# Turning the memory rows of a cross-attention on VectorE and through DRAM, with the norm's root applied behind the projections

## What is computed

```python
def memory_cross_attention(h, m, w_q, w_kv, q_g, k_g, w_o):
    q = rmsnorm(heads(h @ w_q, MEM_HEL2614 TENSOR_TENSOR XL<-SMP,XH 128x4x128 [waits mixed_hi] x2
L2600 TENSOR_TENSOR MGAINED<-MEM,PRE_GAIN 128x512 [waits pre_gain_loaded,mem_loaded]
L2600 TENSOR_TENSOR MGAINED<-MEM,PRE_GAIN 128x512
L2603 STREAM_TRANSPOSE MEM_TURNED_92<-MGAINED 128x4x4x32 [waits mem_gained] x2
L2516 TENSOR_TENSOR XS<-ACCP,XS 128x512 [waits gate_ready,block_done]
...
L2600 TENSOR_TENSOR MGAINED<-MEM,PRE_GAIN 128x512 [waits pre_gain_loaded,mem_loaded]
L2600 TENSOR_TENSOR MGAINED<-MEM,PRE_GAIN 128x512
L2603 STREAM_TRANSPOSE MEM_TURNED_93<-MGAINED 128x4x4x32 [waits mem_gained] x2
L2234 TENSOR_TENSOR LO<-RAW,HI 128x1024 [waits hi_ready,x_again]
...
L2270 SCALAR_TENSOR_TENSOR XS<-X,STAT,POST_GAIN 128x512 [waits xq_gain_loaded,root_ready,acc_taken3,acc_taken2]
L2270 SCALAR_TENSOR_TENSOR XS<-X,STAT,POST_GAIN 128x512
L2674 TENSOR_TENSOR MLO<-MEM_TURNED_92,MH 128x4x128 [waits mem_hi] x2S), q_g)
    k, v = jnp.split(m @ w_kv, 2, axis=-1)
    k = rmsnorm(heads(k, MEM_HEADS), k_g)
    v = heads(v, MEM_HEADS)
    s = jnp.einsum("bqhd,bkhd->bhqk", q, k).astype(jnp.float32) * MEM_DIM ** -0.5
    p = jax.nn.softmax(s, axis=-1).astype(v.dtype)
    o = jnp.einsum("bhqk,bkhd->bqhd", p, v).reshape(B, S, MEM_W)
    return o @ w_o
...
x = x + mixed @ w_out[l]
x = x + memory_cross_attention(rmsnorm(x, norm_xq[l]), rmsnorm(mem, norm_mem[l]), ...)
```

## Time and profile before

| | |
|---|---|
| median of 3 runs | 1126.58 us (1126.37 to 1127.04) |
| the profiled execution | 1127.05 us, of which its span is 1125.1 us |
| PE busy | 1114.9 us, 99% of the span |
| PEld busy | 946.8 us, 84% |
| DVE busy | 766.9 us, 68% |
| ACT busy | 597.0 us, 53% |
| POOL busy | 107.6 us, 10% |
| granted clock of PE, mean | 0.998 of full speed |
| share of PE in the chain that ended last | 93% |

### The profile page before, as it was taken

The page is one execution under the profiler, slowest core; times in us unless marked ns, Lnnn a source line. Parts: engine busy times, 40 slices in busy tenths (PEclk is TensorE's granted clock), DMA queues, the critical chain, the costliest instruction groups (busy, mean ns, idle before and its releaser), DMA issues.

```text
span 1125.1 us, 14628 instructions
## 1 busy us (share of the span) xinstructions
PE 1114.9 (99%) x5637; PEld 946.8 (84%) x5637; DVE 766.9 (68%) x974; ACT 597.0 (53%) x789; POOL 107.6 (10%) x161
## 2 busy tenths in 40 slices
PE   9999999999999999999999999999999999999997
PEld 8998888888888888888888888888888888889886
DVE  6866687657867689894675564666767567655466
ACT  5665555446565477774554443564654365444453
POOL 6410221000011000000000000200500020000020
PEclk9999999999999999999999999999999999999999
DMA  8743653454644798875688775478756668776632
GB/s 252 206 153 113 213 188 129 160 196 168 201 174 151 245 322 281 293 234 176 216 286 250 233 225 201 153 243 251 235 187 220 210 218 279 249 244 215 221 134 76
DMA packets 126550, 236.28 MB, mean 210 GB/s; under 512 B 12961, under 2 KB 44306, under 8 KB 126483
## 3 DMA queue, kind: packets, MB, share of 16 engines
q1 hardware_dynamic: 122881, 224.86, 62.2%
q10 hardware_dynamic: 3506, 10.49, 2.6%
...
## 4 chain that ended last, share of the span: by engine, by line
PE 93%; DVE 3%; DMA 1%; issue 1%; ACT 1%; POOL 0%; POOLq 0%; DVEq 0%; SPq 0%; ACTq 0%
PE ACCP L913 29%; PE ACCP L915 29%; PE ACCP L914 28%; PE SMP L1090 3%; DVE CONVF L2329 2%; DVE LO L2205 1%; PE SMP L1083 1%; DMA RAW<-in_w_in_dram 1%; DMA X<-in_x_dram 0%; PE SMP L1257 0%; PE SMP L1241 0%; PE SMP L1425 0%; DMA POST_GAIN<-in_ple_post_g_dram 0%; PE SMP L1499 0%; PE SMP L1404 0%
## 5 line engine op out<-in xcount | busy, mean ns | idle before, releaser
L2205 DVE TENSOR_TENSOR LO<-RAW,HI 128x1024 fp32r<-128x1024 f32 x365 | 439.2, 1239 | 210.8 <-ACT HI L1601 204.5
L1601 ACT ACTIVATE HI<-RAW 128x1024 fp32r<-128x1024 f32 x366 | 370.8, 1055 | 295.1 <-PE ACCP L915 246.6
L913 PE MATMUL ACCP<-HI,XH 128*128 128x512 f32 (+1 forms) x936 | 365.6, 391 | 0.4 <-DVE XL L2250 0.4
L915 PE MATMUL ACCP<-HI,XL 128*128 128x512 f32 (+1 forms) x936 | 362.8, 388 | 0.0
L914 PE MATMUL ACCP<-LO,XH 128*128 128x512 f32 (+1 forms) x936 | 362.6, 387 | 0.0
L915 PEld LDWEIGHTS ACCP<-HI,XL 128*128 128x128 f32 x936 | 175.8, 188 | 36.0
L913 PEld LDWEIGHTS ACCP<-HI,XH 128*128 128x128 f32 x936 | 175.9, 188 | 35.4 <-issue 0.6
L914 PEld LDWEIGHTS ACCP<-LO,XH 128*128 128x128 f32 x936 | 175.9, 188 | 35.1
L913 PE MATMUL ACCP<-HI,HH 128*128 128x512 f32 x328 | 128.0, 390 | 0.0
L915 PE MATMUL ACCP<-HI,HL 128*128 128x512 f32 x328 | 127.7, 389 | 0.0
L914 PE MATMUL ACCP<-LO,HH 128*128 128x512 f32 x328 | 127.6, 389 | 0.0
...
## 6 DMA issues: line engine op xcount, KB each, us to landing
RAW<-in_w_in_dram SPq DMA_DIRECT2D x104, 512.0 KB, 4.6
RAW<-in_w_up_dram SPq DMA_DIRECT2D x44, 512.0 KB, 5.5
RAW<-in_ffn_w_gate_dram SPq DMA_DIRECT2D x44, 512.0 KB, 4.7
RAW<-in_ffn_w_up_dram SPq DMA_DIRECT2D x44, 512.0 KB, 4.7
RAW<-in_ffn_w_down_dram SPq DMA_DIRECT2D x44, 512.0 KB, 4.5
RAW<-in_w_down_dram SPq DMA_DIRECT2D x22, 512.0 KB, 4.6
scratch_up<-UP_TURNED SPq DMA_DIRECT2D x10, 512.0 KB, 6.4
UP_BLOCKS<-scratch_up SPq DMA_DIRECT2D x40, 128.0 KB, 4.8
```

The source lines that it names most:

```text
L913: pe.matmul(dst, lhs[0], rhs[0], start=start, stop=False)
L915: return pe.matmul(dst, lhs[1], rhs[0], start=False, stop=stop)
L1601: act.activation(HI[:, n % RING, half_of(half)], RAW[:, n % RAWS, half, :], ACT.Copy).then_inc(hi_ready, 1)
L2205: dve.tensor_tensor(LO[:, s, c], RAW[:, n % RAWS, half, :], HI[:, s, c].bitcast(f32), ALU.subtract).then_inc(lo_ready[s], 1)
```

## The change

The change turns the memory rows without PE.

- DVE (`memory_turn(i)`, once for each half i of the 1024 columns) multiplies `MEM` with the weight row alone into `MGAINED` (two operations of 128 x 512) and transposes it in blocks of 32 x 32 into `MEM_TURNED[i]` (two more). `memory_turn(0)` stands ahead of `mix("b", 1)`, `memory_turn(1)` where `norm_scale` of the memory rows was.
- SP writes each `MEM_TURNED[i]` to a scratch in DRAM (`memory_out`) and reads it back in four DMAs (`memory_in`), between the loads of `mem_k` and `mem_q`. `load_d` and `load_t` are written out for that.
- ACT copies `MEM_TURNED[i]` to `MH` (half 0 behind the first `new_square`, half 1 ahead of the second), and DVE subtracts into `MLO` (half 0 behind the first `norm_scale`, half 1 ahead of the second).
- PE loses `turn_memory` and waits on `mem_split` ahead of each block of `mem_k`.
- The root is multiplied in where `MK` and `MV` are copied out of PSUM.
- `MJUNK` moves from 0 to 8 KB of the arena, which leaves 0 to 8 KB to `MEM_TURNED` and 16 to 24 KB to `MGAINED`. `SCALED` is `NORMS` without `norm_mem`, for the counts of two semaphores.

```diff
         MEM = at("MEM", 24, [P, NT, DM])
-        MJUNK = at("MJUNK", 0, [P, NT, DM])
+        MJUNK = at("MJUNK", 8, [P, NT, DM])
+        MGAINED = at("MGAINED", 16, [P, NT, DM])
+        MEM_TURNED = [at(f"MEM_TURNED{i}", 4 * i, [P, 4, NT, 4, 32]) for i in range(2)]
+        mem_rows = [nc.dram_tensor(f"scratch_mem{i}", (4, 32, 4, NT * 128), f32) for i in range(2)]
         MH = at("MH", 32, [P, KT, SEQ], f32r)
...
                     load(f"out_{g}", Turn(j), rows(w[wo], 0, 4, 512 * j, 512))
-            load_d("w_out", w["w_out"])
-            load_t("mem_k", w["w_mkv"], 0)
-            load_t("mem_q", w["w_mq"], 0)
+            def memory_out(i):
+                sp.wait_ge(mem_turned, NT * (i + 1))
+                sp.dma_start(mem_rows[i][:, :, :, :].rearrange("b f q c -> (b f) (q c)"),
+                             MEM_TURNED[i][:, :, :, :, :].rearrange("p q m k t -> p (q m k t)")).then_inc(mem_out[i], 16)
+            def memory_in(i):
+                sp.wait_ge(mem_out[i], 16)
+                for q in range(4):
+                    sp.dma_start(MEM_TURNED[i][32 * q:32 * q + 32].rearrange("p b m k t -> p b (m k t)"),
+                                 mem_rows[i][:, :, q, :].rearrange("b f c -> f b c")).then_inc(mem_in[i], 16)
+            for j in range(4):
+                load("w_out", Turn(j), d_block(w["w_out"], j))
+            memory_out(0)
+            load("mem_k", Turn(0), t_block(w["w_mkv"], 0, 0))
+            memory_in(0)
+            load("mem_k", Turn(1), t_block(w["w_mkv"], 0, 1))
+            memory_out(1)
+            load("mem_q", Turn(0), t_block(w["w_mq"], 0, 0))
+            memory_in(1)
+            load("mem_q", Turn(1), t_block(w["w_mq"], 0, 1))
             load_t("mem_v", w["w_mkv"], HW)
...
             turn_mix(1)
-            def turn_memory():
-                for t in range(NT):
-                    norm_turn("norm_mem", MEM, t)
-            d_tail("w_out", "norm_xq", XH, XL, mixed_is_ready, turn_memory)
+            d_tail("w_out", "norm_xq", XH, XL, mixed_is_ready)
             for j in range(2):
...
                     norm_turn("norm_xq", XS, 1)
-                t_half("mem_k", j, MH, MLO, [norm_ready("norm_mem", m) for m in range(NT)])
+                pe.wait_ge(mem_split, NT * (j + 1))
+                t_half("mem_k", j, MH, MLO)
             t_half("mem_q", 0, XH, XL, [norm_ready("norm_xq", m) for m in range(NT)])
...
                 if between:
-                    between()
+                    between(0)
                 if n >= RING:
...
                 split_ahead(phase, Turn(n - 2))
+                if between:
+                    between(1)
                 new_square(phase, r, 1)
...
-            def memory_split():
+            def memory_split(i):
+                act.wait_ge(mem_in[i], 64)
                 for t in range(NT):
-                    norm_split("norm_mem", t, MH)
+                    copy(MH[:, 4 * i:4 * i + 4, tok(t)].rearrange("p k (b t) -> p k b t", b=4),
+                         MEM_TURNED[i][:, :, t].rearrange("p b k t -> p k b t"), mem_hi)
...
             pre_gain_load("norm_ffn")
-            take_t("mem_k", 0, MK)
+            acc_is_done(act, "mem_k", Turn(0))
+            for m in range(NT):
+                act.wait_ge(root_ready, ROOT_ORDER[f"norm_mem.{m}"] + 1)
+                copy(MK[:, m], acc("mem_k", Turn(0), m), acc_bank("mem_k", Turn(0), m), ROOT[f"norm_mem.{m}"])
             for t in range(NT):
...
             acc_is_done(act, "mem_v", Turn(0))
-            copy(MV[:, 0], acc("mem_v", Turn(0), 0), acc_bank("mem_v", Turn(0), 0))
+            copy(MV[:, 0], acc("mem_v", Turn(0), 0), acc_bank("mem_v", Turn(0), 0), ROOT["norm_mem.0"])
             take_small("mP1a", MPT[:, 0, :, tok(1)], by_head(small("mP1a")))
...
                                          in1=YH[:, :, tok(t)].bitcast(f32), op0=ALU.mult, op1=ALU.subtract).then_inc(bank_of(name), 1)
+            def memory_turn(i):
+                dve.wait_ge(mem_loaded, 16)
+                dve.wait_ge(pre_gain_loaded, 16)
+                part = slice(512 * i, 512 * i + 512)
+                for t in range(NT):
+                    dve.tensor_tensor(MGAINED[:, t, part], MEM[:, t, part], PRE_GAIN[:, part], ALU.mult).then_inc(mem_gained, 1)
+                for t in range(NT):
+                    dve.wait_ge(mem_gained, NT * i + t + 1)
+                    dve.transpose(MEM_TURNED[i][:, :, t].rearrange("p q k t -> p k q t"),
+                                  MGAINED[:, t, part].rearrange("p (k q t) -> p k q t", q=4, t=32)).then_inc(mem_turned, 1)
...
             mixed_split(0)
+            memory_turn(0)
             mix("b", 1)
...
             split_ahead("out_b", Turn(1))
-            for t in range(NT):
-                norm_scale("norm_mem", t, MEM, MEM)
+            memory_turn(1)
...
                 split_ahead(phase, Turn(n - 2), (0,))
+                if r == "norm_xq":
+                    between(2)
                 if behind in T_OPEN:
...
-                norm_split("norm_mem", t, MH, MLO)
+                if t == 0:
+                    return
+                i = t - 1
+                for m in range(NT):
+                    dve.wait_ge(mem_hi, NT * i + m + 1)
+                    part = slice(4 * i, 4 * i + 4)
+                    dve.tensor_tensor(MLO[:, part, tok(m)].rearrange("p k (b t) -> p k b t", b=4), MEM_TURNED[i][:, :, m].rearrange("p b k t -> p k b t"),
+                                      MH[:, part, tok(m)].rearrange("p k (b t) -> p k b t", b=4).bitcast(f32), ALU.subtract).then_inc(mem_split, 1)
...
             acc_is_done(dve, "mem_v", Turn(0))
-            copy(MV[:, 1], acc("mem_v", Turn(0), 1), acc_bank("mem_v", Turn(0), 1))
+            dve.tensor_scalar(MV[:, 1], acc("mem_v", Turn(0), 1), root_is_ready("norm_mem.1"), None, ALU.mult).then_inc(acc_bank("mem_v", Turn(0), 1), 1)
             take_small("mP1b", MPT[:, 1, :, tok(1)], by_head(small("mP1b")))
```

More of the change, by code:

```diff
@@ L152 @@
 SMALL += ["Tt128_0", "Tt128_1", "vn0", "S1", "kS", "qS", "vn1", "o0", "o1", "yT0", "yT1"]
-SMALL += [f"mixT{j}{m}" for j in range(2) for m in range(NT)] + norm_turns("norm_mem") + norm_turns("norm_xq")
+SMALL += [f"mixT{j}{m}" for j in range(2) for m in range(NT)] + norm_turns("norm_xq")
 SMALL += ["mkT0", "mkT1", "mqT0", "mqT1", "mS0a", "mS0b", "mS1a", "mS1b", "mP0a", "mP0b", "mP1a", "mP1b", "mo0", "mo1"]
@@ L163 @@
 SMALL_COUNT = {name: sum(n not in BY_BLOCK for n in SMALL[:i + 1]) for i, name in enumerate(SMALL)}
+SCALED = ["norm_mix", "norm_xq", "norm_ffn", "norm_f1", "norm_mix2", "norm_f2", "norm_ple"]
 NORMS = ["norm_mix", "norm_mem", "norm_xq", "norm_ffn", "norm_f1", "norm_mix2", "norm_f2", "norm_ple"]
@@ L404, in build @@
         gate_ready = sem("gate_ready")
+        mem_gained, mem_turned, mem_hi, mem_split = sems("mem_gained mem_turned mem_hi mem_split")
+        mem_out, mem_in = ([sem(f"mem_{n}{i}") for i in range(2)] for n in ("out", "in"))
         bias_loaded = {g: sem(f"bias_loaded_{g}") for g in "abc"}
@@ L1098, in norm_half_turn @@
             def norm_half_turn(r, source, t, b):
-                pe.wait_ge(scaled, 4 * NORMS.index(r) + 2 * t + b + 1)
+                pe.wait_ge(scaled, 4 * SCALED.index(r) + 2 * t + b + 1)
                 turn_four(f"{r}.{t}{b}", lambda k: source[:, t, (4 * b + k) * P:(4 * b + k + 1) * P])
@@ L2247, in norm_split @@
                     name = f"{r}.{t}{b}"
-                    dve.wait_ge(norm_hi, 4 * NORMS.index(r) + 2 * t + b + 1)
+                    dve.wait_ge(norm_hi, 4 * SCALED.index(r) + 2 * t + b + 1)
                     quarter = slice(4 * b, 4 * b + 4)
```

## The result

The changed kernel took 1129.93 us (median of 9 runs, 1129.4 to 1130.86). The kernel before took 1126.58 in 9 runs beside it (1126.2 to 1127.8). The ratio is 1.003 with an interval of 1.0021 to 1.0038: 3.35 us **slower**, outside the range of 1124.8 to 1127.6. "Within 0.2%" had 90% and was wrong.

A forecast was written before the change was run, and what follows sets the result against it. PE was taken as the bound, with the `XS` chain behind its turns letting only 0.6 of 1.8 us arrive. The sum -0.6 + 0 + 0.05 = -0.55 us took 1126.58 to 1126.0, range 1124.8 to 1127.6.

The forecast's parts named there:

- Within 0.2%: Whole kernel: the forecast case of a time within 0.2% (2.25 us) of the kernel before, given 90%.
- What bounds the kernel: PE, busy 1114.9 of 1125.1 us; behind the turns it meets the `XS` chain over DVE, ACT and POOL.
- part 1: PE loses the turns of `MEM`: -1.8 us of work on PE, with nothing replacing them.
- Part 2, the calls on DVE: `memory_turn` calls of about 2.5 us; the mix comes 1.0 us later with 1.5 of cover, costing nothing now.
- Part 3, tile 0: First `XS` turn: scaling starts 0.77 us earlier, PE waits about 0.1 and 0.4; 1.25 of 1.8 us left.
- Part 4, tile 1: Second `XS` turn: scaling at 303.25, 0.64 us earlier; PE waits, and some 0.6 of 1.8 us arrive.
- Part 5, the load of `X`: `X` shares DMA engines with half 0's read-back: keeps its share and lands as before, 0; at worst 1.4 us later.
- Part 5, the round trip: DRAM write 6.4 us, reads 4.8: half 0 back by 288.5, 4 us spare; half 1 taken as 298.5, free until 299.7.
- a late half 1 makes the kernel slower: Rival: ACT waits for half 1 before tile 1's square; gain gone from 300.3, slower past 302.6, up to 1131; 7%.
- `X` lands late: Rival: tile 0's chain moves with `X`; gain gone at 0.6 late, loss of 0.8 at 1.4; 1126.0 to 1127.4; 17%.
- Part 6: Root in the copies of `MK` and `MV` out of PSUM: 0.05 to 0.1 us longer each; +0.05 through `MV`.
- What would show it: Signs: PE waits 0.3 to 0.6 us at both `XS` turns; wrong if `X` lands past 288.3 or ACT waits for `MEM_TURNED`.

The follow-up runs named there:

- e7: Changed kernel with DVE's memory pairs in waits, half 0 back before `X` loads, half 1 written after, `LO` before `X` wait, second `MLO` pair later; 1125.67 us.
- e6: Changed kernel with half 0's read-back behind both `mem_k` loads, `memory_turn(0)` behind `mix("b", 1)`, second `MLO` pair behind tile 1's scaling; 1127.72 us.
- e2: Changed kernel without the read-back of half 0; write, transposes and half 1 stay; 1127.1 us.
- e3: Changed kernel with half 0 read back by one DMA in 4 KB rows instead of four in 1 KB rows, same place and bytes; 1129.01 us.
- e12: The changed kernel measured once more, unaltered; 1129.81 us.
- e1: Changed kernel with the read-back of half 0 issued behind all loads of `mem_k` instead of ahead of the second; 1127.33 us.
- e8: Changed kernel with the `LO` of the first `mem_k` block ahead of DVE's wait for `X`; 1127.95 us.
- e11: Changed kernel with two of half 0's four reads ahead of the load of `X` and two behind `mem_k`'s second load; 1128.73 us.

## Why the prediction was wrong, point by point

**What bounds the kernel, and part 1.** Right. The turns cost PE 1.8 us, a chain without slack stands behind them, and what the change does to the chain decides. In e7, where the chain keeps up, the median falls by 1.0 us, with an interval that just includes no change.

**Part 2, the calls on DVE.** The length was right (272.56 to 275.07 for 2.5). "It costs nothing now" was wrong by 0.56 us. I asked who wants the data of the mix (the turns of `X`, 1.5 us of cover) and didn't ask who wants the PSUM banks that the mix reads. PE wants them at 276.6, 2.7 us ahead of the turns.

**Part 3, tile 0.** Right in size. From `add_residual` to the scaling it was 4.35 us before and is 3.62 after: 0.73 earlier, 0.77 forecast.

**Part 4, tile 1.** From `add_residual` to the scaling I had 3.71 us; it is 4.33 after, 3.58 before. The term for the new pair on `MLO` counted DVE's time only. The pair runs beside the root and POOL's two small operations take 0.75 us longer. The rows read for POOL showed 0.57 with nothing beside it. The Trainium skill, SBUF — State Buffer, section SBUF: two separate sides, says that a DVE operation with two inputs in SBUF and a GpSimd operation that reads SBUF exclude each other. The pair reads PSUM before the change and SBUF after, and e6 agrees with this: 1.62 us beside it, 0.88 without.

**Part 5, the load of `X`: the step that failed.** I took 0 for it, since SP's queue had had work in this window before as well, and 1.4 as the bound. It was 3.3 us, 3.0 of it the way of `X`. I had assumed that a kept share keeps the landing. From 284 to 287 ACT's queue had even more of the engines' time than before (72.2% against 52.6%) and moved hardly more (0.69 MB against 0.63), and it moved 0.27 MB less than in e2, where no small rows stood beside it. The bound fell too, since it priced bytes: e3 comes near that price (1.5), the four DMAs with 1 KB rows cost 2.1 to 3.0. The Trainium skill, DMA: Bandwidth & Descriptors, section Queues, rings and completion order, from which I had that an engine takes turns between queue rows packet by packet, is not contradicted: 169 packets against 216 in those 3 us are in keeping with it. What I drew from it was that `X` lands as before, and that does not follow when the engines' packets carry fewer bytes.

**Part 5, the round trip.** Right in that it cost no wait: ACT took half 1 at 301.85 without waiting. But I had the write of half 0 landing after 6.4 us, by 282, and its reads issued behind that and so behind the load of `X`. The write had landed within 5.3 us (275.09 to the issue at 280.41), and the reads went out ahead of `X`. The rival that a late half 1 makes the kernel slower named the right kind of cause, new DMAs in a crowd, at the wrong transfer. "`X` lands late", 17%, was the right one, but capped at +0.8, and so the range ended at 1127.6.

**What stood nowhere in the prediction.** The low clock. It is 1.6 us of the 3.8, and it makes waits of 3.5 us (3.21 ahead of the first turn, 0.28 in its middle) cost 5.1. The forecast had only waits up to 0.6 us.

**Part 6.** Right: the copies of `MV` last 0.69 and 0.75 instead of 0.60 and 0.69. The groups of instructions from 330 to 372 in the kernel after (busy us, mean ns of one, idle before and its releaser):

```profile
L2702 DVE TENSOR_SCALAR MV<-ACCP,STAT 128x512 f32<-128x512 f32 x1 | 0.8, 750 | 0.6 <-PE ACCP L941 0.6
L1626 ACT ACTIVATE MV<-ACCP,STAT 128x512 f32<-128x512 f32 x1 | 0.7, 688 | 1.2 <-PE ACCP L941 1.2
```

**What would show it.** One sign of being wrong came true: `X` landed past 288.3, at 291.0. PE did not resume near 295.5 but at 299.08. ACT didn't wait for `MEM_TURNED`.

**What stays open.** How the DMA engines serve the two queues (e3 against e12 speaks against a price by bytes alone). A price by packets is a lead, an estimate and not tested: at the 128 packets per us of 284 to 287, 512 rows of 1 KB would take 4.0 us and 128 rows of 4 KB 1.0, where 2.1 to 3.0 and 1.5 were measured. Why e1 and e8 have medians some 1 us above what their best executions show. Whether two short-rowed reads ahead of `X` delay it as much as four do, as the one profiled execution of e11 has it.
